# A chunkwise delta-rule recurrence on one core: the whole 64 x 64 inverse, four bursts of small products a chunk instead of five, and the last token tile of two heads transposed later

## The chip, the cores and the metric

One NeuronCore of one Trainium2 chip. The metric is the device time of one execution of the whole program in microseconds; the kernel before takes 772.99 us, the median of three runs (772.95 to 773.49). TensorE (PE in the rows; PEld is its weight load) does the products, VectorE (DVE) and ScalarE (ACT) the elementwise work and the reading of PSUM, SyncE (SP) and GpSimd (POOL) issue transfers. All arithmetic named here is float32; one float32 product shows as two instructions in the trace.

## The reference, cut to what matters

One layer of a decoder with two mixer branches (RWKV-7 and retention) and a hierarchical mixture of experts, for 528 prompt tokens (16 meta tokens and 512) and 8 sample tokens. The change touches the RWKV-7 recurrence over the prompt and the place of one small step of the retention branch:

```python
def rwkv_recurrence(r, w, k, v, kk, a, s0):
    def step(S, inp):
        r_t, w_t, k_t, v_t, kk_t, a_t = inp
        sa = jnp.einsum('bhvk,bhk->bhv', S, -kk_t)
        S = (S * w_t[:, :, None, :] + sa[..., None] * (kk_t * a_t)[:, :, None, :]
             + v_t[..., None] * k_t[:, :, None, :])
        y = jnp.einsum('bhvk,bhk->bhv', S, r_t)
        return S, y
...
scores = jnp.einsum('bihd,bjhd->bhij', q, k) * decay[None]
intra = jnp.einsum('bhij,bjhv->bihv', scores, v)
```

There are 8 RWKV heads of 64 channels and 4 retention heads of 128.

## The kernel before, in words

`order()` (from line 270) writes out one list of steps, `STEPS`, and each engine walks this list and does its own share of every step, in the list's order. So a step's place in the list is its place in the queue of every engine.

**The recurrence** works in chunks of 64 tokens (`CHUNKS`: eight full chunks and a last one of 16). Within a chunk the sequential rule becomes a triangular system: `sa` = (I - L)^-1 times a right side `rr`, with L strictly lower triangular, 64 x 64 for each head. The kernel inverts only the two 32 x 32 diagonal blocks (d = 0 and 1) of every head, by levels of doubling size: `wk_x` (line 1654) multiplies and `wk_t` (line 1667) updates, at levels 2, 4, 8 and 16, and after each of them DVE masks or adds the result from PSUM. The 8 heads x 2 blocks make 16 products of 32 x 32 for one `wk_x`. The block below the diagonal enters by substitution: `wk_sa` (1694) solves the upper half, `wk_y` (1704) multiplies it by the block below the diagonal (`below`), DVE adds that to `rr`, and `wk_sb` (1715) solves the lower half. `wk_r` (1681) makes the right side, `wk_s` (1723) the new state and the outputs, `wk_a` (1605) the chunk's score matrices, `wk_d` (1622) the raw diagonal blocks, `wk_k` (1638) the transposes. `wk_p` 0 to 5 (line 2393) are DVE's preparations of a chunk, `wk_e` three exponentials on ACT.

**Bursts and takes.** `bursts(c)` (line 360) groups the small products into five bursts for each chunk c, each with the work of c and of the one or two chunks ahead of it. Between two bursts stand `TAKES` = 3 pieces of large work ("takes"): halves of the gate and branch products at 128 x 128 x 260 (`j_f` at line 1438, `j_bb` at line 1415, in the first chunks `j_proj` at line 1402), some with DVE sums of weights (`fs`) ahead of them. `between` spreads the chunk's DVE and ACT steps over the takes. The loop starts at c = -2 with six takes ahead of it and two after each burst (`TAKES_AHEAD`), which is where the levels of chunks 0 and 1 are worked off, with the four sums `tg` of 128 x 1040 on DVE and eight small jobs `j_bon` of the bonus term.

**The retention heads** run earlier, behind the slots of a seven-product scheme (`j_w`, eight instructions at line 1457 for each slot, `seven(n, ...)`). Head h's steps stand at slots counted from `HEADS[h]` = 12, 22, 32, 42. `j_vt` and `j_kt` (1524) transpose the first four token tiles of v and k; `j_t4` (1518 to 1520) transposes the last, 24 rows with the last 16 prompt tokens and the 8 samples. `j_t4` waits for the rotated keys of its head (`rope`, on DVE, at the slots of `TURNS`: heads 0 to 3 at 7, 19, 31 and 39). It stands at slots 12, 22, 32 and 40. ACT reads its result, then POOL carries the sample rows out and back (`v_dram`, `v_all`) for `rs_v` on DVE at slots 18, 28, 38 and 46, and SP writes keys and values out (`kept`). These small jobs use PSUM banks 4 and 5 in turn: one may open when the last job but one has been read.

## Time and profile before

| | before |
|---|---|
| median of 3 runs | 772.99 us (772.95 to 773.49) |
| profiled execution | 773.59 us, span of its trace 771.9 us |
| PE busy | 740.1 us, 96% |
| DVE busy | 428.4 us, 56% |
| ACT busy | 229.5 us, 30% |
| retention heads and projections | about 26 to 254 us of the span |
| recurrence with the gate products between | about 257 to 503 us |
| branch and output products, routing | 503 to 619 us |
| experts, last rows | 619 to 772 us |

The page gives busy shares and the span in slices; the waits list who stood idle for whom; the timeline gives start and duration of merged instructions in order. A busy PE is not PE at its peak, since small products overlap and their latency counts as busy: so the cost of a group of small products is read from its start to the start of the next group.

### The profile page before, as it was taken

To read this page: it belongs to the slowest core of one execution; us is meant where nothing else is said; L and a number is where in the kernel's file an instruction comes from. 1 tells how busy PE (TensorE), PEld (TensorE's weight loads), DVE (VectorE), ACT (ScalarE), POOL (GpSimd) and SP (SyncE) were. 2 spreads that over 40 slices of the span, in tenths; PEclk is the share of its full clock that TensorE was granted. 3 is DMA by queue.
4 is the path that set the end of the run, shared out by engine and by line. 5 is a ranking of instruction groups with operands and counts; after the bars stand their busy time and mean duration, and the time that the engine had idled before them with its cause. 6 is when DMAs were issued, how large, how long until landed. Compare 5 with 4: busy or idle time off the path is not lost.

```text
span 771.9 us, 19753 instructions
## 1 busy us (share of the span) xinstructions
PE 740.1 (96%) x8328; PEld 527.0 (68%) x8328; DVE 428.4 (56%) x862; ACT 229.5 (30%) x543; POOL 45.3 (6%) x53
## 2 busy tenths in 40 slices
PE   7999999999999999999999999999999699999995
PEld 5887787787778777778878878778887533333331
DVE  5956667788787675756565564465223442212146
ACT  5122222254523333333323344310031501111145
POOL 0000000000000000010000000000000112221221
PEclk9999999999999999999999999999999689999998
DMA  9562432531221101121442102183934789999965
GB/s 324 205 207 85 155 126 72 209 114 56 73 91 56 56 30 58 58 59 44 148 119 59 57 30 84 44 332 122 409 125 167 250 349 397 392 402 390 377 211 220
DMA packets 38135, 130.43 MB, mean 169 GB/s; under 512 B 6267, under 2 KB 16763, under 8 KB 33184
## 3 DMA queue, kind: packets, MB, share of 16 engines
q1 hardware_dynamic: 32544, 115.07, 40.1%
q0 software_dynamic: 5504, 14.10, 6.2%
q8 instruction: 67, 1.10, 0.6%
q14 instruction: 20, 0.16, 0.1%
HBM read 111.13 MB, written 18.66 MB: 168 GB/s over the span
## 4 chain that ended last, share of the span: by engine, by line
PE 86%; DVE 5%; DMA 4%; issue 2%; ACT 1%; POOL 0%; SPq 0%; POOLq 0%; DVEq 0%; ACTq 0%
PE psum L1457 23%; PE psum L1812 11%; PE psum L1438 11%; PE psum L2784 9%; PE psum L2818 4%; PE psum L1415 4%; DVE arena L2184 3%; PE psum L1402 2%; PE psum L1390 2%; PE psum L1664 1%; PE psum L2764 1%; PE psum L1678 1%; PE psum L1580 1%; PE psum L1675 1%; DMA u_rows<-arena 1%
## 5 line engine op out<-in xcount | busy, mean ns | idle before, releaser
L2184 DVE TENSOR_TENSOR arena<-arena 128x268 f32<-128x268 f32 (+13 forms) x322 | 176.5, 548 | 47.6 <-ACT arena L1911 28.3
L1457 PE MATMUL psum<-arena 128*128 128x268 f32 x784 | 188.4, 392 | 0.0
L1457 PEld LDWEIGHTS psum<-arena 128*128 128x128 f32 x784 | 145.6, 190 | 33.0 <-issue 6.7
L1911 ACT ACTIVATE arena<-psum 128x268 f32<-128x268 f32 (+7 forms) x207 | 83.0, 410 | 258.9 <-PE psum L1457 138.6
L1911 ACT ACTIVATE arena<-arena 64x256 f32<-64x256 f32 (+11 forms) x173 | 69.0, 430 | 104.1 <-PE psum L1824 57.7
L1438 PE MATMUL psum<-arena 128*128 128x260 f32 x392 | 96.9, 392 | 0.8 <-DVE arena L2184 0.6
L2184 DVE TENSOR_TENSOR arena<-psum,arena 128x256 f32<-128x256 f32 (+7 forms) x151 | 60.4, 405 | 55.5 <-PE psum L1678 12.4
L1812 PE MATMUL psum<-arena 128*128 128x260 f32 x384 | 88.3, 385 | 1.5 <-DVE arena L2184 0.8
L2784 PE MATMUL psum<-arena 128*32 128x512 f32 (+1 forms) x640 | 86.7, 604 | 0.5 <-DVE arena L2949 0.3
L1438 PEld LDWEIGHTS psum<-arena 128*128 128x128 f32 x392 | 70.9, 189 | 17.3 <-issue 5.4
L1812 PEld LDWEIGHTS psum<-arena 128*128 128x128 f32 x384 | 71.3, 190 | 15.4 <-DVE arena L2187 2.1
L2949 DVE TENSOR_TENSOR arena<-psum,arena 128x256 f32<-128x256 f32 (+2 forms) x38 | 24.3, 663 | 102.1 <-ACT arena L2853 90.7
L2784 PEld LDWEIGHTS psum<-arena 128*32 128x32 f32 (+1 forms) x640 | 25.4, 117 | 58.2 <-issue 57.6
L2187 DVE SCALAR_TENSOR_TENSOR arena<-arena 128x536 f32<-128x536 f32 (+9 forms) x77 | 48.9, 635 | 7.7 <-ACT arena L1911 3.2
L2818 PE MATMUL psum<-arena 128*32 128x512 f32 (+1 forms) x288 | 40.2, 596 | 0.0
L2187 DVE SCALAR_TENSOR_TENSOR arena<-psum,arena 128x260 f32<-128x260 f32 (+2 forms) x23 | 10.2, 442 | 45.7 <-PE psum L1812 40.2
L1415 PE MATMUL psum<-arena 128*128 128x260 f32 x128 | 31.5, 390 | 0.0
L2184 DVE TENSOR_TENSOR arena<-arena,psum 128x260 f32<-128x260 f32 (+4 forms) x35 | 17.6, 514 | 20.5 <-PE psum L1438 16.8
L2853 ACT ACTIVATE arena<-psum 128x256 f32<-128x256 f32 x12 | 4.6, 384 | 78.8 <-PE psum L2784 78.8
L2187 DVE SCALAR_TENSOR_TENSOR arena<-arena,psum 128x260 f32<-128x260 f32 x32 | 13.7, 427 | 24.7 <-PE psum L1415 15.0
L1415 PEld LDWEIGHTS psum<-arena 128*128 128x128 f32 x128 | 23.2, 189 | 4.4 <-issue 0.4
L2818 PEld LDWEIGHTS psum<-arena 128*32 128x32 f32 (+1 forms) x288 | 10.8, 115 | 21.3 <-issue 21.3
(233 smaller groups left out, 669.0 us busy)
## 6 DMA issues: line engine op xcount, KB each, us to landing
arena<-in_w_gu SPq DMA_DIRECT2D x16, 2048.0 KB, 19.7
arena<-in_w_in SPq DMA_DIRECT2D x45, 512.0 KB, 4.2
arena<-in_w_dn SPq DMA_DIRECT2D x16, 1024.0 KB, 17.2
arena<-in_w_out SPq DMA_DIRECT2D x2, 2048.0 KB, 14.9
arena<-in_x SPq DMA_DIRECT2D x8, 268.0 KB, 6.0
arena<-arena SPq DMA_DIRECT2D x16, 134.0 KB, 4.4
arena<-in_x SPq DMA_DIRECT2D x1, 2144.0 KB, 14.5
arena<-arena SPq DMA_DIRECT2D x4, 520.0 KB, 6.5
```

The costliest lines, as they stand in the source:

```text
L1390: last = mm(ps, wt[:, i, k, :], xg[:, k, cols(hf)], start=(k == 0), stop=(k == KD - 1))
L1402: last = mm(ps, fill_in(0)[side][:, k // 2, k % 2, :], u[:, k, cols2(hf)], start=(k == 0), stop=(k == KD - 1))
L1415: last = mm(ps, bb_tile(m)[:, k, :], ret_o[:, k, cols2(hf)], start=(k == 0), stop=(k == NP - 1))
L1438: last = mm(ps, w[:, k // 2, k % 2, :], x[:, k, :], start=(k == 0 and i in (0, 1, 3)), stop=(k == KD // 2 - 1), skip_group_check=i not in ...
L1457: last = mm(ps, w[:, k, :], x[:, k, :], start=(k == 0 and i in (0, 1, 3)), stop=(k == KD // 2 - 1), skip_group_check=i not in (0, 1, 3))
L1812: last = mm(ps, w[:, k, :], x[:, k, cols2(hf)], start=(k == 0), stop=(k == nk - 1))
L1911: run(nc.scalar.activation(out, in_, fn, **kw), s)
L2184: run(v.tensor_tensor(out, a, b, op), s)
L2187: run(v.scalar_tensor_tensor(out, a, sc_, b, op0, op1), s)
L2784: last = mm(bank(2 + i % 2)[part], ue[:, i % 2, k, part], w_gu[x % NWE][:, k, :], start=(k == 0), stop=(k == KD - 1))
L2818: last = mm(bank(down_bank(e) + q)[part], hht(e)[:, f, part], w_dn[x % NWE][:, f, 512 * q:512 * q + 512], start=(f == 0), stop=(f == 1))
L2949: v.tensor_tensor(out, x, y, op).then_inc(s, 1)
```

## The change

In the recurrence the inverse becomes the whole 64 x 64 matrix. A fifth `wk_x` (level 32) multiplies the block below the diagonal by the upper inverse, a new step `wk_u` multiplies the lower inverse by that, and ACT assembles the pieces in `inv` (`wk_w` copies the two diagonal blocks in four instructions, `wk_u` the lower left one in two). `wk_sa` then solves a whole chunk with products of 64 x 64 x 64; `wk_y` and `wk_sb` and DVE's addition are gone. For full chunks `wk_t` at level 16 also keeps the other form of the upper block (eight more products). The bursts are regrouped into four for a chunk, with takes 4, 4, 3, 4 between them; the first levels of a chunk start one chunk earlier, the loop starts at c = -3 and `xl` and the PSUM places of `wk_x` and `wk_t` have two copies by the chunk's parity, so that PE no longer waits between two `wk_x` of one burst. DVE reads PSUM of `wk_x` or `wk_t` only after the last such product of the burst (and after `wk_d`, where it is in the burst). `wk_p` 0 to 4 of chunk c + 3 stand behind bursts 0 and 1 of chunk c, and `wk_d` of c + 3 in burst 2. In the heads, `j_t4` moves from slot 22 to 24 (head 1) and from 40 to 41 (head 3).

```diff
-TAKES = (3, 3, 3, 3, 3)
-TAKES_AHEAD, TAKES_LAST = 2, (3, 3, 2, 2, 2)
+TAKES = (4, 4, 3, 4)
+TAKES_FIRST, TAKES_AHEAD, TAKES_LAST = 4, 2, (3, 3, 2, 3)
...
-        then(b - 2 if h == RH - 1 else b, ("j_t4", h))
+        then((b, b + 2, b, b - 1)[h], ("j_t4", h))
...
-        return [of(c, ("wk_t", 16)) + of(c + 1, ("wk_x", 4)) + of(c, ("wk_r",)) + of(c + 1, ("wk_k",)),
-                of(c + 1, ("wk_t", 4)) + of(c, ("wk_sa",)),
-                of(c, ("wk_y",)) + of(c + 2, ("wk_d",)) + of(c + 1, ("wk_x", 8)),
-                of(c + 1, ("wk_t", 8)) + of(c + 2, ("wk_x", 2)) + of(c, ("wk_sb",)) + of(c + 1, ("wk_a",)),
-                of(c + 2, ("wk_t", 2)) + of(c + 1, ("wk_x", 16)) + of(c, ("wk_s",))]
+        return [of(c, ("wk_r",)) + of(c + 2, ("wk_x", 2)) + of(c + 1, ("wk_x", 8)) + of(c, ("wk_x", H)) + of(c + 1, ("wk_a",)),
+                of(c, ("wk_u",)) + of(c + 1, ("wk_t", 8)) + of(c + 2, ("wk_t", 2)),
+                of(c, ("wk_sa",)) + of(c + 1, ("wk_x", 16)) + of(c + 2, ("wk_x", 4)) + of(c + 3, ("wk_d",)),
+                of(c, ("wk_s",)) + of(c + 1, ("wk_t", 16)) + of(c + 2, ("wk_t", 4)) + of(c + 2, ("wk_k",))]
...
-    s += take(6)
-    for c in range(-2, len(CHUNKS) - 1):
+    s += take(TAKES_FIRST)
+    for c in range(-3, len(CHUNKS) - 1):
...
+        between = [of(c + 3, ("wk_e",)) + (prep(c + 2, ("wk_p", 5)) if c + 2 else []) + of(c + 1, ("wk_b",), ("wk_m",), ("wk_l",))
+                   + prep(c + 3, ("wk_p", 0)),
+                   prep(c + 3, ("wk_p", 1), ("wk_p", 2), ("wk_p", 3), ("wk_p", 4)),
+                   so[0:1], of(c + 1, ("wk_v",), ("wk_w",)) + so[1:3]]
+        for i, x in {-2: ((2, 0), (3, 1)), -1: ((1, 2), (2, 3))}.get(c, ()):
+            between[i].append(("tg", x))
...
                     for p, s, d, g, rd in tiles_of(c):
-                        last = mm(psum[g, 2304 + H * p:2304 + H * p + n], ad[c % 2][g, p, 0:n], tp[c % 3][g, 0, p, 0:n],
-                                  start=True, stop=True)
+                        if b == H:
+                            if d == 0:
+                                last = mm(psum[64 * s + H:64 * s + 64, 2560 + H * p:2560 + H * p + H], below[g, p, :],
+                                          tp[c % 3][g, 0, p, :], start=True, stop=True)
+                            continue
+                        o = 2304 + 128 * (c % 2) + H * p
+                        last = mm(psum[g, o:o + n], ad[c % 2][g, p, 0:n], tp[c % 3][g, 0, p, 0:n], start=True, stop=True)
...
+                elif kind == "wk_u":
+                    c = step[1]
+                    pe.wait_ge(s_xl, X_N[(c, H)])
+                    for p, s, d, g, rd in tiles_of(c):
+                        if d == 1:
+                            last = mm(psum[64 * s:64 * s + H, 3840 + H * p:3840 + H * p + H], tp[c % 3][g, 0, p, :],
+                                      tp[c % 3][g, 1, p, :], start=True, stop=True)
+                    last.then_inc(s_py, 1)
...
+                    if CHUNKS[c][1] == C:
+                        pe.wait_ge(s_y1, 6 * (c + 1))
+                        for p in range(NP):
+                            for s in range(2):
+                                _, _, full, _ = wk(c, s)
+                                last = mm(psum[full, 3328 + 64 * p:3328 + 64 * p + 64], inv[full, p, :], rr[full, p, :],
+                                          start=True, stop=True)
...
-                    dve.wait_ge(s_pt, X_N[(c, b)])
+                    dve.wait_ge(s_pt, X_RUN[(c, b)][1])
+                    for x in burst_of(step):
+                        if x[0] == "wk_d":
+                            dve.wait_ge(s_pab, PAB[x])
```

## Rows read from the trace of the kernel before

**Rows 1.** The page: busy time of PE and DVE, share of the span, instructions.
```profile
PE 740.1 (96%) x8328; PEld 527.0 (68%) x8328; DVE 428.4 (56%) x862; ACT 229.5 (30%) x543; POOL 45.3 (6%) x53
```
**Rows 2.** Windows: length, busy time by engine, granted clock, DMA share, GB/s.
```profile
306.00:503.00 197.00, 194.88 (x4270) 156.89 (x4264) 116.12 (x259) 70.47 (x183) 6.74 (x13) 1.00 0.23 70
619.00:738.00 119.00, 118.53 (x908) 42.09 (x908) 27.01 (x54) 15.89 (x27) 23.94 (x19) 0.98 0.97 376
```
**Rows 3.** Waits of PE: who waited for whom, us in total, times, longest.
```profile
PE psum L1520 <- issue: 3.0, 2, 1.5
PE psum L1678 <- DVE arena L2184: 1.1, 1, 1.1
```
**Rows 4.** Timeline of PE in chunks 4 and 5: start, duration, instructions, count.
```profile
388.35 0.68 PE L1742 MATMUL psum<-arena 64*64 64x64 f32 x16
388.96 2.90 PE L1415 MATMUL psum<-arena 128*128 128x260 f32 x12
391.79 0.45 PE L1678 MATMUL psum<-arena 32*32 32x32 f32 x32
392.07 0.48 PE L1664 MATMUL psum<-arena 32*32 32x32 f32 x32
...
397.32 0.64 PE L1701 MATMUL psum<-arena 32*32 32x64 f32 x16
397.90 2.90 PE L1438 MATMUL psum<-arena 128*128 128x260 f32 x12
400.73 0.64 PE L1712 MATMUL psum<-arena 32*32 32x64 f32 x16
401.29 0.45 PE L1631 MATMUL psum<-arena 64*32 64x32 f32 x32
```
**Rows 5.** The chain that ended last: a long run of large products without bursts.
```profile
254.92 4.38 PE psum L1402 x20
```
**Rows 6.** Timeline of chunk 5: DVE's work and the wait of PE behind it.
```profile
404.15 2.15 DVE L2184 TENSOR_TENSOR arena<-arena 128x512 f32<-128x512 f32 x3
404.99 1.12 PE L1438 MATMUL psum<-arena 128*128 128x260 f32 x4 [0.61 <-DVE arena L2184]
```
**Rows 7.** Timeline of the ahead stage: PE's waits, and the sums of 1040.
```profile
263.16 0.72 PE L1601 MATMUL psum<-arena 128*128 128x268 f32 x2 [0.26 <-DVE arena L2184]
276.46 1.23 DVE L2184 TENSOR_TENSOR arena<-arena 128x1040 f32<-128x1040 f32 x1
288.88 0.45 PE L1678 MATMUL psum<-arena 32*32 32x32 f32 x32 [1.10 <-DVE arena L2184]
```
**Rows 8.** Groups on DVE, 260 to 500 us: count, busy us, mean ns, idle before.
```profile
L2184 DVE TENSOR_TENSOR arena<-psum,arena 128x256 f32<-128x256 f32 x48 | 20.3, 426 | 27.9 <-PE psum L1678 10.5 <-PE psum L1742 8.5 <-PE psum L1664 4.4
L2184 DVE TENSOR_TENSOR arena<-psum,arena 128x128 f32<-128x128 f32 x45 | 13.2, 293 | 5.8 <-PE psum L1678 1.9 <-PE psum L1664 1.8 <-PE psum L1620 0.6
```
**Rows 9.** Timeline around `j_t4` of heads 2 and 3, with `rope` on DVE.
```profile
95.17 0.72 DVE L2184 TENSOR_TENSOR arena<-arena 128x536 f32<-128x536 f32 x1
95.99 0.60 PE L1520 MATMUL psum<-arena 128*24 128x128 f32 x4 [1.53 <-issue]
...
118.68 0.60 PE L1520 MATMUL psum<-arena 128*24 128x128 f32 x4 [1.43 <-issue]
122.28 0.55 POOL L1337 DMA_DIRECT2D arena<-v_smp  x1 [1.29 <-DMA v_smp<-arena]
...
134.31 1.22 DVE L2184 TENSOR_TENSOR arena<-arena 128x1024 f32<-128x1024 f32 x1
```
**Rows 10.** The page: a slot of the seven-product scheme is eight of these.
```profile
L1457 PE MATMUL psum<-arena 128*128 128x268 f32 x784 | 188.4, 392 | 0.0
```
**Rows 11.** Timeline around `j_t4` and `j_kt` of head 1.
```profile
68.01 0.62 PE L1520 MATMUL psum<-arena 128*24 128x128 f32 x4
...
73.23 0.60 PE L1524 MATMUL psum<-arena 128*128 128x128 f32 x4
73.49 1.07 DVE L2184 TENSOR_TENSOR arena<-psum,arena 128x256 f32<-128x256 f32 x2 [0.45 <-PE psum L1554]
```

More of the change, by code:

```diff
@@ L2064, in _ @@
                         act.wait_ge(s_act, own[0])
-                elif kind == "wk_b" and CHUNKS[step[1]][1] > H:
+                elif kind == "wk_b":
                     c = step[1]
@@ L2353, in _ @@
                 elif kind == "st0":
+                    for i in range(2):
+                        run(v.memset(inv[64 * i + H:64 * i + C, :, 0:H], 0.0))
                     job_done(dve, ("j_w", len(PAIRS) - 1, SEVEN - 1))
```

154 lines of the change are left out of this document (77 added, 77 removed).

## The prediction

> **What bounds the kernel now.** The first look is the page: PE is busy 96% of the span, DVE 56% [rows 1]. The second is the windows, because a share of the whole hides stages: in the recurrence, 306 to 503 us, PE is busy 194.9 of 197.0 us at a granted clock of 1.00 and DVE 116.1 [rows 2]. The third is the list of waits of PE. Before 600 us it holds few entries, and two bear on this change: 3.0 us in two waits at line 1520, which is `j_t4`, and 1.1 us at line 1678, `wk_t`, behind DVE [rows 3]; single waits of 0.61 and 0.26 us behind DVE stand in the timeline [rows 6, 7]. So the recurrence is bound by what PE has to push through, not by the chain of dependences: the five bursts and fifteen takes of a chunk follow each other nearly without a gap. A change there is worth what it takes off PE's queue, less the waits that it makes. A step counts from its start to the next start, since the durations of small products overlap: 32 instructions of 32 x 32 last 0.45 us by the record, but the next group starts 0.28 us later [rows 4].
>
> **The change part by part.** The time is summed against the profiled span of 771.9 us; that execution took 773.59 us, 0.6 above the median of 772.99, to which the difference is applied.
>
> (1) Products removed, for each of the eight full chunks. `wk_sa` on the upper half is 16 instructions of 32 x 32 x 64, from 397.32 to 397.90, 0.58 us. `wk_y` has the same shape, 400.73 to 401.29, 0.56 us. `wk_sb` has it too, and I take it at the same 0.56 [rows 4]. Together 1.70 us.
>
> (2) Products added, for each of the same chunks. The new `wk_sa` has 16 instructions of 64 x 64 x 64, the shape of line 1742: 388.35 to 388.96, 0.61 us [rows 4]. Level 32, `wk_u` and the extra half of `wk_t` at level 16 are 16 instructions of 32 x 32 x 32 each, on two of the four row groups. No row shows such a half group. From below: half the instructions of a full group, half of its 0.28 us, 0.14. From above: each row group works off its own eight instructions one after the other, as in the full group, so the half group takes as long, 0.28. The row that it is nearest to is line 1701, also 16 instructions on two row groups, with twice the columns: half of its 0.58 is 0.29 [rows 4]. I take 0.28, so three cost 0.84 (0.42 from below). Added: 0.61 + 0.84 = 1.45 us.
>
> At this place the Trainium skill speaks against the change. In "TensorEngine Tiling (Array Packing)", section Restrictions and Gotchas, it says that different row tiles cannot access the same PSUM bank simultaneously; all products of one of these groups write one bank. By that the sixteen would run one by one. The row stands against it: 32 products' instructions on four row groups go to one bank in 0.28 us, 9 ns each, where one large instruction of 260 columns takes 219 ns, so that 32 columns in their share of it would alone be 27 ns; four together are needed to come to 9 [rows 4, 5]. By the rule the three half groups would cost 3 x 16 x 27 ns = 1.30 us instead of 0.84 and the sum would be 3.7 us smaller; the measurement decides, and I leave it out.
>
> (3) One burst fewer. Twelve large instructions without a burst take 12 x 4.38 / 20 = 2.63 us [rows 5]. Between two bursts they take 391.79 - 388.96 = 2.83 and 400.73 - 397.90 = 2.83 [rows 4]. So each change from small products to large and back costs 0.20 us; the number of large instructions is the same (15 takes a chunk before and after). Minus 0.20 us a chunk. Changes of shape inside the bursts are about as many as before and are left at nothing, with 0.1 a chunk to either side in the range.
>
> (1) to (3): -1.70 + 1.45 - 0.20 = -0.45 us a chunk, eight times: -3.6 us. With half groups at 0.14 it is -0.87 a chunk, -7.0 us.
>
> (4) DVE and ACT in the recurrence. DVE loses one addition of 128 x 256 (426 ns) a chunk and gains a copy of 128 x 128 (293 ns), and the level-16 update is 256 instead of 128 wide (+133 ns) [rows 8]: no change. ACT loses two reads and gains four short copies and two more, hidden, since it is busy 70.5 of 197 us [rows 2] and they stand a burst ahead of who needs them: `wk_w` is queued on ACT behind the last take of burst 3, ahead of the read of `wk_r`, which PE needs only in burst 2. That cover would have to shrink from about 10 us to under 2 to cost anything. The distances between the links of the chain (`wk_r`, `wk_sa`, `wk_s`, back to `wk_r`) grow from three takes to eight, three and four. What gets closer is `wk_d` of chunk c + 3: it waits for `wk_p` 4 of that chunk, which DVE meets only behind the last take of burst 1. Ahead of `wk_d` PE has in burst 2 `wk_sa`, `wk_x` 16 and `wk_x` 4, 0.61 + 0.28 + 0.28 = 1.17 us; DVE has in that time the subtraction or product of the take and `wk_p` 4, two operations of 0.43 with a gap, about 1.0 us. It is covered, by little. Then DVE waits in burst 2 for `wk_d` before it reads `wk_x` 16, and behind it queue `wk_x` 4, the three operations of `wk_d` and the next sums `fs`. A wait of PE for such sums exists already, 0.61 us behind three operations of 128 x 512 [rows 6]. Such waits I take as many as before; bounds -0.8 (the 0.61 goes and none comes) and +3 us (one of 0.4 us in each of seven chunks).
>
> (5) The ahead stage. It has eight bursts with two takes each where it had nine, -0.2 us; the number of takes ahead of the first `wk_r` is 4 + 2 + 8 + 8 = 22, as before (6 + 6 + 10). DVE is closer to full here: behind burst 1 of c = -1 stand four `wk_p` (4 x 0.43), a `tg` of 1.23 us and two `wk_t` (2 x 0.43), 3.8 us with the gaps near 4.2, in a stretch of PE of about 1.2 us of burst and 2 to 2.6 us of takes. So `wk_d` of chunk 2 is late by some 0.5 us, and at c = -2 `wk_d` of chunk 1 and a `j_bon` behind it by some 1.1 us together. Against that goes the wait of 1.10 us at line 1678 in the old order, and the 0.26 stays [rows 7]. Net +0.5 us; bounds -1.1 and +2.
>
> (6) `j_t4`. PE waits at it for heads 2 and 3, 1.53 and 1.43 us, and for head 1 not at all [rows 9, 11]. At head 2 the rotation of the keys ends on DVE at 95.89 and PE starts at 95.99. The diff leaves head 2 where it is. Head 3 moves one slot of eight large products back, 8 x 188.4 / 784 = 1.92 us [rows 10], more than the 1.43; the rotation then is done, and PE's bank has been read. Gain 1.43 us; bounds 0 (the wait goes to the next small job) and -1.5. It is past no queue that has no room: POOL sent the samples' rows out at 122.28 and the product that needs them runs on DVE at 134.31, 12 us later, of which two go [rows 9]. SP's `kept`, its two writes, comes later by the same and ahead of loads that are asked for two pairs early. Head 1 moves from slot 22, where it cost no wait, to 24, between a score and `j_kt`. With the bank order then `j_kt` opens on the score's bank. DVE starts to read that score at 73.49, ends at about 73.92, and `j_kt` could start at about 73.75 [rows 11]: +0.2 us; bounds 0 and +0.5.
>
> **Sum:** -3.6 + 0 - 0.2 + 0.5 - 1.43 + 0.2 = -4.5 us. I take -4.2, since in (4) a little more can come than go: 773.0 - 4.2 = 768.8 us. What follows, to the end of the routing, is bound by PE as well or starts from PE's steps. The experts' stage has DMA at 0.97 with PE busy 118.5 of 119.0 us [rows 2]: its loads start when PE frees their buffers, so they move with PE, and the gain is kept.
>
> **The rivals.** A, the half groups are cheap: 0.14 us each, -0.87 a chunk; -7.0 - 0.2 + 0.5 - 1.4 + 0.2 + 0.3 gives 765.4 us. For it speaks that 32 instructions need no longer than 0.28 us; against it line 1701.
>
> B, the gain is eaten by new waits behind DVE in bursts 0 to 2 and in the ahead stage, at their upper bounds in part: +3 us against -4.2 gives 771.8 us, no difference that a measurement of this kernel tells from none (0.2%, 1.5 us). For it speaks that DVE is busy 59% of the stage and that its reads now wait for the last product of a burst; against it, that its longest lag in the steady chunks shows once.
>
> C, slower: `wk_d` waits for `wk_p` 4 in every chunk. The place is burst 2. If DVE reaches `wk_p` 4 one operation of 128 x 512 (0.7 us) later than I have it, and the operations behind it (`wk_x` 16, three of `wk_d`, `fs`) push the wait on to a take, PE loses 0.7 us at `wk_d` and about 0.3 behind it, nine times: +9 us against -4.2 gives 777.8. It decides from 0.6 us a chunk on: there nine waits are worth 5.7 us, the 4.2 and the 1.5 of the bound. Against it: DVE's total is not raised.
>
> D, the change doesn't do what it says at the heads: the wait of head 3 goes elsewhere, to the score or `j_ros` behind it, and head 1 costs 0.5: +1.7, 770.5 us. It lies in the forecast's range.
>
> **How the numbers follow.** The forecast with D in it has 0.57, A 0.15, B 0.17, C 0.11. Faster by over 0.2% (under 771.4 us) are the forecast and A: 0.72, less 0.01 for the forecast's edge; within 0.2%: B and the edge, 0.17; slower 0.12. The range: A at 765.4 reaches to about 764.8 with a tenth beyond; on the other side B is inside and most of C outside, 773.5.
>
> **What would show it.** The timeline of a steady chunk: `wk_sa` of 64 x 64 from start to next start 0.6 us; `wk_u` 0.28 (A: 0.14); twelve or sixteen large instructions 0.2 us above 0.219 each; the period of a chunk 0.45 us shorter. In PE's waits: line 1520 with one wait of 1.5 instead of two; line 1524 new with 0.2; waits at line 1631's successor (`wk_d`) behind DVE under 0.3 us in sum in the steady chunks (C: 0.7 each). The prediction is wrong if PE's waits behind DVE or ACT between 254 and 503 us come to over 5 us, or if a new step waits for instructions rather than for data.

## The result: 23 us slower, and the profile after

The changed kernel takes 795.93 us (median of four runs, 791.96 to 798.99) beside 772.97 us for the kernel before on the same chip (four runs, 772.35 to 773.49): 1.0293 times the time, 95% interval 1.0261 to 1.0324. The prediction was 768.8 us in a range of 764.8 to 773.5. Its profiled execution is its longest run, 798.99 us, with a span of 797.3 us; before it was 771.9 us. The 25.4 us between the two spans are what the traces have to account for. Three single executions that took 1.6 times as long or more (one of the run with a take inside the burst, two of the kernel before) are left out of all medians and ratios below.

The page of the changed kernel, the rows for PE and DVE and the two that carry instructions (queue, kind, packets, MB, share):

```profile
PE 748.4 (94%) x8456; PEld 532.6 (67%) x8456; DVE 429.0 (54%) x864; ACT 237.0 (30%) x575; POOL 44.9 (6%) x53
...
q8 instruction: 68, 1.11, 0.6%
q14 instruction: 20, 0.16, 0.1%
```

DVE works as long as before [rows 1]; PE is busy for a smaller share of a longer span. The windows (length, PE busy, granted clock, DMA share, GB/s) of the stage ahead and of the recurrence:

```profile
254.00:306.00 52.00, 47.10 (x1153) 1.00 0.13 39
306.00:503.00 197.00, 181.77 (x4099) 0.97 0.23 68
```

In the recurrence PE stands idle for 15.2 of 197 us where it was 2.1 [rows 2], and the clock is 0.97 where it was 1.00. For whom it waits there, 254 to 530 us, in total, times, longest (the largest entries):

```profile
PE psum L1635 <- issue: 5.4, 4, 1.6
PE psum L1665 <- issue: 3.0, 2, 2.6
PE psum L1698 <- issue: 2.7, 1, 2.7
PE psum L1432 <- ACT arena L1926: 2.0, 1, 2.0
PE psum L1646 <- DVE arena L2215: 2.0, 2, 1.7
PE psum L1455 <- DVE arena L2212: 0.9, 1, 0.9
PE psum L1683 <- DVE arena L2458: 0.9, 1, 0.9
PE psum L1455 <- issue: 0.8, 1, 0.8
```

Most of it is "issue", 12.6 of 20.5 us: no semaphore ended it. Line 1635 is `wk_a`, 1662 and 1665 are `wk_k`, 1694 and 1698 `wk_t`, 1646 and 1650 `wk_d`, 1679 and 1683 `wk_x`, 1432 and 1455 are takes. The timeline shows what is odd about these stalls (start, duration, line, operation, shape, count, idle before):

```profile
404.23 0.63 PE L1662 MATMUL psum<-arena 128*64 128x128 f32 x4
404.69 0.49 PE L1665 MATMUL psum<-arena 128*128 128x128 f32 x3
407.80 0.33 PE L1665 MATMUL psum<-arena 128*128 128x128 f32 x1 [2.62 <-issue]
407.97 3.70 PE L1432 MATMUL psum<-arena 128*128 128x260 f32 x16
411.60 0.69 PE L1719 MATMUL psum<-arena 128*64 128x64 f32 x16
412.21 0.75 PE L1683 MATMUL psum<-arena 32*32 32x32 f32 x64
412.82 0.44 PE L1679 MATMUL psum<-arena 32*32 32x32 f32 x16
413.19 0.94 PE L1635 MATMUL psum<-arena 64*128 64x128 f32 x12
415.29 0.49 PE L1635 MATMUL psum<-arena 64*128 64x128 f32 x4 [1.16 <-issue]
```

They fall inside a step: between the third and fourth instruction of `wk_k`'s second half, behind the twelfth of sixteen of `wk_a`. In the code no wait stands inside these loops, so no data is awaited there.

A count over the trace says where they fall. All records of PE's stream are numbered from 0, in order of time: matmuls, weight loads and the 535 waits and other instructions of its sequencer. Each product in this kernel's code is four (two loads, two matmuls), a transpose two. By these numbers the stalls of over 0.3 us that the list calls "issue" end, from 254 to 530 us, at 193 or 194 above a multiple of 256. Instructions come in packets of 16384 bytes (1.11 MB in 68 packets on queue 8, above). The stream has 17,447 records; 68 packets of 256 instructions would be 17,408, at 64 bytes each, so queue 8 is read here as PE's. The packets' times beside the times at which PE passes these places ("borders"), taken from the records of the trace. These are nine of the borders; where there is a stall, the time is its end:

```
passed at us   line   us since the last fetch began   us until the next began   stall there
 364.13        1694   4.23                            1.82                      -
 369.41        1683   3.46                            1.16                      -
 374.42        1757   3.85                            0.23                      -
 377.17        1665   2.53                            5.60                      0.35
 385.14        1635   2.37                            1.24                      1.56
 402.62        1757   2.43                            2.57                      -
 407.80        1665   2.61                            4.85                      2.62
 415.29        1635   2.64                            1.75                      1.16
 435.52        1455   2.46                            4.66                      0.84
```

Over all twenty traces of this case there are 111 such stalls between 254 and 530 us, of 0.3 to 4.2 us. All end at 193 to 195 above a multiple of 256, though the kernels' streams differ, and each ends 2.2 to 3.2 us behind the beginning of a fetch. The two waits at `j_t4` that the list also calls "issue" end at other numbers (126 and 99 in the kernel before). So PE stands still for its own instructions. It does so at one border in eight: PE passes some 890 in these stretches, and in the changed kernel nine of 44 have a stall. In a burst of small products PE goes from border to border in some 2 to 3 us (402.62 to the stall behind 404.69 above), a fetch needs 2.2 to 3.2 us to be of use, and the next one begins behind a border, 0.2 to 2.8 us in most cases; right behind a burst's end, with takes following, it began 4.7 to 5.6 us later. In the kernel before the same list had two entries of the kind, which I had read past:

```profile
PE psum L1652 <- issue: 1.1, 1, 1.1
...
PE psum L1675 <- issue: 0.5, 1, 0.5
```

The Trainium skill, "Runtime: NRT & Kernel Launch", section Instruction fetch mechanics, says that instructions are refilled in blocks of 256 and that the sequencer fetches the next page while it executes the current one. The packets agree. It also says that crossing such a boundary is mostly hidden. By count that is so here (35 of the 44 borders), but the nine others cost 0.3 to 2.7 us each, 12.6 us together.

The second part of the loss is the clock. Around the stall at 304.8 to 307.6 us, and behind it:

```profile
306.00:308.00 2.00, 0.44 (x22) 0.75 0.86 281
308.00:313.00 5.00, 5.00 (x17) 0.50 0.13 37
```

PE was idle for 2.72 us, and the granted clock goes to 0.50, that is 1.2 instead of 2.4 GHz; the takes in it run at half speed. The same stands behind the stall at 443.10:

```profile
443.10 0.49 PE L1635 MATMUL psum<-arena 64*128 64x128 f32 x3 [1.34 <-issue]
443.51 4.58 PE L1432 MATMUL psum<-arena 128*128 128x260 f32 x12
```

Twelve large instructions take 4.58 us where they took 2.90 [rows 4]. The kernel before has no such stretch in the recurrence. The changed kernel has three there, 13.7 us together, and one of 3.4 us at 98.80 us, in the heads' stage, behind the wait of 1.5 us at head 2's `j_t4` that the kernel before has too [rows 9].

**The sum**, from the records of both traces. Idle time is that between PE's first and last instruction. "At borders": idle stretches of PE of over 0.25 us at the places above, 254 to 530 us. "Half speed": half of the time at 0.50, which is what it costs if PE has work all the while. "Rest": span less this idle time less half speed, that is PE's work at the full clock and some 14 us ahead of PE's first instruction and behind its last. The differences are of the unrounded values.

| us | before | after | difference |
|---|---|---|---|
| idle at borders, 254 to 530 us | 1.5 | 12.6 | +11.1 |
| other idle time, 254 to 530 us | 4.6 | 7.8 | +3.3 |
| idle elsewhere | 11.4 | 14.3 | +2.8 |
| half speed | 12.4 | 20.8 | +8.5 |
| rest | 742.0 | 741.7 | -0.3 |
| span | 771.9 | 797.3 | +25.4 |

Of the half-speed term 6.8 us belong to the recurrence and 1.7 to the stretch at 98.80 us. The idle time elsewhere grew behind 530 us, in the routing and at the experts' first products; why is open.

### The profile page after: what moved, and what is told of

It is laid out like the page before. It is cut to its first block, busy times and chain, and to the rows that moved or that the text cites. A ratio compares the mean times of both kernels' runs of the same rounds, so it can differ in the third digit from the quotient of the medians.

```text
span 797.3 us, 20050 instructions
## 1 busy us (share of the span) xinstructions
PE 748.4 (94%) x8456; PEld 532.6 (67%) x8456; DVE 429.0 (54%) x864; ACT 237.0 (30%) x575; POOL 44.9 (6%) x53
## 3 DMA queue, kind: packets, MB, share of 16 engines
q8 instruction: 68, 1.11, 0.6%
## 4 chain that ended last, share of the span: by engine, by line
PE 81%; DVE 6%; DMA 5%; issue 4%; ACT 3%; SPq 0%; POOL 0%; POOLq 0%; DVEq 0%; ACTq 0%
PE psum L1474 20%; PE psum L1455 11%; PE psum L1827 11%; PE psum L2817 9%; DVE arena L2212 4%; PE psum L1432 4%; PE psum L2851 3%; DMA arena<-u_rows,ids 2%; PE psum L1407 2%; PE psum L1698 1%; PE psum L1683 1%; ACT arena L1926 1%; PE psum L1635 1%; PE psum L2797 1%; PE psum L1694 1%
## 5 line engine op out<-in xcount | busy, mean ns | idle before, releaser
L2212 DVE TENSOR_TENSOR arena<-arena 128x268 f32<-128x268 f32 (+12 forms) x322 | 176.5, 548 | 48.3 <-ACT arena L1926 28.5
L1474 PEld LDWEIGHTS psum<-arena 128*128 128x128 f32 x784 | 146.6, 191 | 33.9 <-issue 7.0
L1926 ACT ACTIVATE arena<-psum 128x268 f32<-128x268 f32 (+7 forms) x223 | 87.5, 400 | 267.0 <-PE psum L1474 140.4
L1926 ACT ACTIVATE arena<-arena 32x128 f32<-32x128 f32 (+9 forms) x205 | 78.2, 410 | 119.4 <-PE psum L1839 57.7
L1455 PE MATMUL psum<-arena 128*128 128x260 f32 x392 | 99.9, 403 | 1.8 <-DVE arena L2212 0.9
L2212 DVE TENSOR_TENSOR arena<-psum,arena 128x128 f32<-128x128 f32 (+6 forms) x143 | 58.3, 411 | 70.4 <-PE psum L1698 14.2
L1827 PE MATMUL psum<-arena 128*128 128x260 f32 x384 | 88.3, 385 | 1.5 <-DVE arena L2212 0.8
L1455 PEld LDWEIGHTS psum<-arena 128*128 128x128 f32 x392 | 74.0, 196 | 17.8 <-issue 5.7
L1827 PEld LDWEIGHTS psum<-arena 128*128 128x128 f32 x384 | 71.2, 189 | 15.5 <-DVE arena L2215 2.1
L1432 PE MATMUL psum<-arena 128*128 128x260 f32 x128 | 32.9, 405 | 2.0 <-ACT arena L1926 2.0
L1432 PEld LDWEIGHTS psum<-arena 128*128 128x128 f32 x128 | 24.5, 199 | 7.1 <-ACT arena L1926 2.4
L2215 DVE SCALAR_TENSOR_TENSOR arena<-arena,psum 128x260 f32<-128x260 f32 x32 | 13.7, 427 | 26.8 <-PE psum L1432 17.1
## 6 DMA issues: line engine op xcount, KB each, us to landing
arena<-in_w_out SPq DMA_DIRECT2D x2, 2048.0 KB, 15.2
arena<-in_x SPq DMA_DIRECT2D x1, 2144.0 KB, 15.6
```

The source lines that it names most:

```text
L1432: last = mm(ps, bb_tile(m)[:, k, :], ret_o[:, k, cols2(hf)], start=(k == 0), stop=(k == NP - 1))
L1455: last = mm(ps, w[:, k // 2, k % 2, :], x[:, k, :], start=(k == 0 and i in (0, 1, 3)), stop=(k == KD // 2 - 1), skip_group_check=i not in ...
L1474: last = mm(ps, w[:, k, :], x[:, k, :], start=(k == 0 and i in (0, 1, 3)), stop=(k == KD // 2 - 1), skip_group_check=i not in (0, 1, 3))
L1827: last = mm(ps, w[:, k, :], x[:, k, cols2(hf)], start=(k == 0), stop=(k == nk - 1))
L1926: run(nc.scalar.activation(out, in_, fn, **kw), s)
L2212: run(v.tensor_tensor(out, a, b, op), s)
```

## The experiments

Theory F: PE starves for instructions at the borders, and the clock falls behind some of the stalls. Rival D: the stalls belong to the new steps themselves (banks, row tiles, a wait that the trace misattributes). Later the question was how much is the longer bursts (B) and how much the place where the borders fall (P); L says that the kernel before had a lucky place.

### The instruction stream moved: empty instructions

```diff
+            for _ in range(64):          # 128, 192 in the others
+                pe.nop(nofuse=True)
             pe.wait_ge(s_set, 1)
```

> The changed kernel with 64 empty instructions at the head of TensorE's program, where it waits for the first loads anyway; nothing else differs. Theory (blocks): TensorE's instructions come in blocks of 256 (queue 8 moved 68 packets and 1.11 MB, 16 KB each), all long waits marked issue end at the same place modulo 256, and a block that is used up in the time of a dense burst, under about 3.5 us, is followed by a wait for the next. A chunk of the changed kernel has 5 blocks of instructions almost exactly, so the two bad borders (in wk_k and in wk_a) come back in every chunk. Shifted by 64 only one border a chunk should be bad: 783 to 790 us, waits in wk_a at lines 1635 to 1637 gone. Rival (dependences: semaphores, a busy VectorE): nothing moves, 792 to 799 us.

> As the one before with 128 empty instructions. Theory (blocks): the waits move to other lines, about two borders a chunk are bad again (inside burst 2 and in the first half of burst 3): 790 to 800 us, but none of the waits in wk_a. Rival (dependences): the same waits at the same lines, 792 to 799 us.

> As the one before with 192 empty instructions. Theory (blocks): waits move again, to burst 1 and burst 2, 786 to 800 us. Rival (dependences): no change, 792 to 799 us. If the three shifts and the changed kernel lie within 2 us of each other, the theory of blocks is wrong.

Measured: 795.55, 792.91 and 795.12 us; 1.0305 (1.027 to 1.034), 1.0295 (1.024 to 1.035), 1.0301 (1.026 to 1.034). The empty instructions appear nowhere in the traces, and every stall ends at the number it had. So nothing was shifted, and these runs say nothing on the theories, though their numbers fit the rivals. They are of use as repeats of the changed kernel. The third of them and the changed kernel (span and granted clock):

```profile
core 0: 788.0 us, clock 0.988
```
```profile
core 0: 797.3 us, clock 0.975
```

The order of instructions is the same, PE's idle time too (35.0 and 34.7 us in all), but the first spent 20.6 us at half speed and the second 41.6. Half of the 21.0 is 10.5 us, and the spans differ by 9.3. So the spread of the changed kernel's runs is mostly the clock, and not each stall brings a half-speed stretch: this run has none in the recurrence, with nearly the same stalls (11.3 us at borders beside 12.6).

### One half alone: the two heads

The kernel before with only the places of `j_t4` changed.

```diff
-        then(b - 2 if h == RH - 1 else b, ("j_t4", h))
+        then((b, b + 2, b, b - 1)[h], ("j_t4", h))
```

> The kernel before with only the new places of j_t4 (heads 1 and 3). The prediction's step: minus 1.4 us for head 3, plus 0.2 for head 1, 771.8 us. Rival: the wait of head 3 goes to another job, 772.5 to 773.2. The theory of blocks: no instruction is added, two waits may be, so the phase of the recurrence stays and nothing of the 23 us shows here.

Measured: 773.66 us, 1.0004 (0.9989 to 1.0020). Its waits of PE from 60 to 254 us:

```profile
PE psum L1520 <- issue: 1.5, 1, 1.5
PE psum L1524 <- DVE arena L2184: 0.5, 1, 0.5
PE psum L1573 <- DVE arena L2184: 0.4, 1, 0.4
```

Head 3's 1.43 us at line 1520 are gone [rows 3, 9], and `j_kt` of head 1 (1524) waits 0.5 us for DVE. That leaves 0.9 us, less than this comparison can tell from none.

### The stream moved in truth: additional small products

Each product is four instructions in PE's stream, so n additional ones ahead of the first step move all that follows by 4n places.

```diff
                         pe.wait_ge(s_sq, KD * hf + k + 1)
+                        for _ in range(32 if (hf, k) == (0, 0) else 0):     # 64 in the other
+                            mm(ps[0:H, 0:1], ones[:, 0:H], squares[:, 0, 0:1], start=True, stop=True)
                         for i in range(4):
```

The expectations count two instructions for each product; the shifts were 128 and 256 places, as the numbers of the stalls show, not 64 and 128 as written in them.

> The changed kernel with 32 additional one-column matmuls (64 instructions, about 0.6 us) ahead of the first matmul of the norm's first step, so that every later instruction of TensorE stands 64 places further in its stream. The empty instructions of the runs before did not appear in the stream, so this is the first real shift. Theory F (TensorE starves for instructions: all unexplained stalls end at the same place of a block of 256 instructions, behind a late instruction fetch): the borders of the blocks now fall 64 instructions earlier in each chunk, in the middle of the t4 step with another border 256 dense instructions ahead of it, and at the end of the group of x steps. One bad border a chunk is left where there were two: the stalls move to other steps (the end of t4 instead of k and wk_a), their sum in 290 to 475 us falls from about 15 us to 6 to 10, and the time is 784 to 791 us. Rival D (the stalls belong to the steps: shared PSUM banks, row tiles of the half groups, or a wait for data that the trace misattributes): same steps, same lengths, 793 to 799 us.

Measured: 796.34 us, 1.0294 (1.0265 to 1.0323). PE's waits, and one of them in the timeline:

```profile
PE psum L1652 <- issue: 10.6, 5, 2.6
```
```profile
398.18 0.39 PE L1652 MATMUL psum<-arena 64*32 64x32 f32 x21
401.16 0.31 PE L1652 MATMUL psum<-arena 64*32 64x32 f32 x11 [2.59 <-issue]
401.40 4.58 PE L1432 MATMUL psum<-arena 128*128 128x260 f32 x12
```

(Line 1652 here is line 1650 of the changed kernel, `wk_d`.) The stalls left `wk_k` and `wk_a` and went to `wk_d`, which had none in the steady chunks, in five chunks; a sixth stands in `wk_t`. Their numbers in the stream are 5570, 6850, 8130, 9410, 10689 and 10946: still 193 or 194 above a multiple of 256.

> The changed kernel with 64 additional one-column matmuls at the same place (128 instructions, about 1.2 us): all later instructions stand 128 places further. Theory F: no burst now holds two borders, and no border stands right ahead of the takes; the unexplained stalls in 290 to 475 us fall from about 15 us to 2 to 6, none of them in wk_a or k, and the clock has no stretch at half speed in the recurrence; 778 to 787 us. Rival D: same steps and lengths as in the changed kernel, 794 to 800 us.

Measured: 797.65 us, 1.0312 (1.0273 to 1.0352):

```profile
PE psum L1637 <- issue: 4.9, 4, 1.6
PE psum L1667 <- issue: 2.6, 1, 2.6
PE psum L1700 <- issue: 2.2, 1, 2.2
```

Moved by one whole block the stalls are back in the steps and at nearly the sizes of the changed kernel (lines 1635, 1665, 1698 there), 10.0 us together. That is what F says of 256 places, and D cannot say why 128 should empty these steps and 256 fill them. D is out. F's forecasts of time missed all the same: 784 to 791 and 778 to 787 us were expected. That of fewer stalls, made for a shift of 128, is answered by the run before, where the sum at the borders stayed 11.9 us; a shift of 64 in truth comes below.

### Five bursts instead of four

```diff
-TAKES = (4, 4, 3, 4)
+TAKES = (3, 3, 3, 3, 3)
...
-                of(c, ("wk_s",)) + of(c + 1, ("wk_t", 16)) + of(c + 2, ("wk_t", 4)) + of(c + 2, ("wk_k",))]
+                of(c, ("wk_s",)) + of(c + 2, ("wk_k",)), of(c + 1, ("wk_t", 16)) + of(c + 2, ("wk_t", 4))]
```

(from chunk 0 on; `TAKES_LAST` is (3, 2, 2, 2, 2))

> The changed kernel, all its steps and sums as they are, but its last burst (s, t16, t4, k: about 336 instructions of TensorE) split in two: s and k, then three takes, then t16 and t4, with three takes behind each of the five bursts instead of 4, 4, 3, 4. Theory F: the longest run of dense instructions falls from 336 to about 290; two fetches in a burst disappear; stalls without a releaser in 290 to 475 us fall from about 15 us to 2 to 7, and the time is 775 to 785 us (the additional burst costs 0.2 us in each of 8 chunks). Rival D: the same sum of stalls, 794 to 800 us. Rival W (the waits for VectorE and ScalarE are the loss): these were 5 us in the changed kernel; fewer takes between dependent steps raise them, over 800 us.

Measured: 787.37 us, 1.0179 (1.0145 to 1.0214); borders 3.6 us. The stalls are within F's 2 to 7 us, the time is 2.4 us above its range. Rival W (over 800 us) is out. The rest looked like F's case, until the same kernel was moved by 128 places with the additional products:

> The kernel with five bursts, and 32 one-column matmuls (128 instructions, 0.6 us) ahead of the norm's first, so that the borders of the blocks of 256 instructions lie half a block away from where they lay. It has no burst over 290 instructions. Theory F: the 2.2 us stall in the stage ahead (t at 306.8 us, right behind a late fetch) and the 0.5 to 0.9 us ones at wk_a and t leave those places; others of 0.5 to 2.5 us may come where a border now falls behind a late fetch; their sum in 290 to 475 us stays at 2 to 7 us, far under the 15 us of four bursts: 781 to 790 us. If the phase were what made five bursts cheap (rival P), the stalls would come back to 10 us or more: over 792 us.

Measured: 794.16 us, 1.0272 (1.025 to 1.0294); borders 9.7 us, where F had 2 to 7. The rival P had set 792 as its mark: the place of the borders, not the five bursts, had made most of the gain.

### The recurrence alone

The changed kernel with the old places of `j_t4`.

> The changed kernel with the last token tile of heads 1 and 3 transposed at its old place: the inverse and the bursts alone. The heads alone made 1.0004 of the time of before, so by every theory this is the changed kernel's time within 0.4%: 792 to 799 us; that the two parts work on each other (the head's steps move where the blocks of instructions end) would show as a difference over 3 us.

Measured: 795.09 us, 1.0289 (1.0256 to 1.0322). The whole loss is the recurrence's.

### The same mechanism in the kernel before

The kernel before with 32 additional products of one column in each chunk: all ahead of x16 in the longest burst, or 16 ahead of x4 and 16 ahead of x8.

```diff
                     n = min(CHUNKS[c][1], H)
+                    for p, s, d, g, rd in tiles_of(c)[0:4] * (8 if b == 16 else 0):     # (4 if b in (4, 8) else 0)
+                        mm(psum[g, 2304:2305], ad[c % 2][g, 0, 0:n], tp[c % 3][g, 0, 0, 0:1], start=True, stop=True)
                     for p, s, d, g, rd in tiles_of(c):
```

> The kernel before, with 32 additional one-column products of 32 x 32 tiles (128 instructions of TensorE; their results are overwritten by the step's own) ahead of the x16 step of each chunk, in its longest burst (t2, x16, s: about 291 instructions, then about 419). None of the change is in it. The work added is 8 chunks x 32 products x about 20 ns = 5 us. Theory F (TensorE's instruction fetch: a burst in which a whole block of 256 instructions is used up faster than the next is fetched starves): of 8 bursts of 419 instructions about five hold two borders of blocks, each with a stall of 1 to 2.7 us that no releaser ends, inside s or x16; 773 + 5 + 5 to 13 = 783 to 791 us. Rival D (stalls belong to the new kernel's steps or banks): 5 us of work and no stall, 777 to 779 us.

> The control of the run before: the same 32 products in each chunk, 16 ahead of x4 in the first burst (181 to 245 instructions) and 16 ahead of x8 in the third (227 to 291), so that no burst is longer than the kernel before has one already. The same work, 5 us. Theory F: stalls as few as in the kernel before (1.6 us in two), or up to 3 us: 777 to 781 us, and at least 5 us under the dense one. Rival D: equal to the dense one within 1 us.

Measured: dense 803.0 us, 1.0395 (1.037 to 1.042); spread 790.91 us, 1.0224 (1.020 to 1.0248). The waits of the dense one:

```profile
PE psum L1744 <- issue: 6.7, 2, 4.2
PE psum L1733 <- issue: 3.2, 1, 3.2
PE psum L1739 <- issue: 2.5, 1, 2.5
PE psum L1666 <- issue: 1.3, 1, 1.3
```

Lines 1733 to 1744 are `wk_s`, a step that the change does not touch, behind x16 in the lengthened burst. So the kernel before, without anything of the change, falls into the same stalls (14.3 us at borders) once work is added to its burst, and the same work put elsewhere costs 12 us less. The 12 us are not the price of the longer burst alone: each run shows one place of the borders, and the place by itself is worth more than that in other kernels (below). Both took more than F's figure (783 to 791, and 777 to 781). In the spread one the borders cost 7.7 us (up to 3 us were expected), the half-speed term 13.9, and the rest is 748.9, that is 6.9 us above before for the added work where I had 5. No burst was over 291 instructions there, as in the kernel before: that length alone is no limit under which nothing happens.

### A take inside the longest burst

```diff
-            s += now_
+            inside = int(i == 3 and 0 <= c < len(CHUNKS) - 2 and c != 5)
+            s += now_[:1] + take(1) + now_[1:] if inside else now_
```

(and one take fewer behind that burst)

> The changed kernel with one of the four takes behind its last burst of chunks 0 to 4 and 6 moved into that burst, behind s: no additional work, the same order of all else, the same place in the instruction stream from the burst's end on. Theory F: the stalls inside that burst (k 2.6, 0.7 and 0.4 us, t16's 2.7 us is of the stage ahead and stays) go, as a take of 0.9 us lies between its two borders; those of wk_a in the next burst (1.2 to 1.6 us, four times) have their border where they had it, three takes behind k's end instead of four, and stay or grow: stalls without a releaser in 315 to 475 us fall from about 10 to 4 to 8 us, 789 to 794 us. Rival P (phase alone decides, not the dense run): k's stalls stay, 793 to 799 us.

Measured: 794.84 us (median of three), 1.0279 (1.025 to 1.0308); the borders cost 9.4 us instead of 12.6:

```profile
PE psum L1636 <- issue: 4.8, 4, 1.9
PE psum L1699 <- issue: 2.7, 1, 2.7
PE psum L1663 <- issue: 1.9, 1, 1.9
```

`wk_k`'s stall did not go, as F had it, but stands at 1.9 us, and `wk_a`'s stayed. The stalls of 315 to 475 us sum to 6.7 us, inside F's 4 to 8, and the time is within P's 793 to 799. But the kernels with the same recurrence and nothing moved scatter as much: 6.4 to 9.5 us in that window, with `wk_k`'s largest stall at 1.2 to 2.4 (the empty instructions, the recurrence alone). So this run decides nothing. One take of 0.9 us inside is less than the fetch's delay.

### How much is the place of the borders

From one `wk_s` to the next PE's stream has 1276 or 1277 records in the changed kernel, nearly five blocks (1280), so a border stands in the same step of one chunk after the other: the stalls in `wk_a` are at 7362, 8641, 9922 and 11202. In the kernel before it is 1243 to 1245, and the borders drift by some 36 a chunk. These runs move both kernels by 64, 128 or 192 places with the additional products (16, 32 or 48 of them).

> The kernel before with 16 one-column matmuls (64 instructions, 0.3 us) ahead of the norm's first: nothing else is changed. Its chunk has about 1250 instructions, so the borders of the blocks of 256 drift by some 30 from chunk to chunk and meet each place of a burst at most once or twice. Theory F: its two small stalls (1.1 and 0.5 us) go or move, others of that size may come: 772 to 777 us. If the kernel before merely had a lucky phase (rival L), it loses 5 us or more: over 778 us.

> The same with 32 one-column matmuls (128 instructions, 0.6 us). Theory F: 772 to 778 us; rival L: over 778 us.

> The changed kernel with 16 one-column matmuls at the same place (64 instructions): the borders lie in its last burst twice a chunk, about 20 instructions behind its beginning and 256 later, in t4's second half. Its chunk is 5 x 256 instructions, so that is so in each chunk. Theory F: stalls of 2 to 2.7 us without a releaser at the end of t4 or at k in four or five chunks, none in wk_a; 10 to 14 us between 290 and 475 us, 792 to 798 us. If this were the lucky phase (rival L), less than 5 us of stalls and under 786 us.

> The changed kernel with 48 one-column matmuls (192 instructions): the borders lie twice in its second burst (u, t8, t2: 290 instructions), at its beginning and near its end. Theory F: stalls of 2 to 2.5 us in t2's second half in four or five chunks, none in k or wk_a; 8 to 14 us between 290 and 475 us, 789 to 797 us. Rival L: under 786 us.

> The kernel with five bursts, moved by 64 instructions. With shifts of 0 and 128 it took 787.4 and 794.2 us, the changed kernel with its four bursts 796 and 796, and 785.9 and 808.4 with shifts of 64 and 192. If the four longer bursts cost time of themselves (B), five bursts are below four in the mean over the four phases, by 5 us or more: 780 to 788 us here. If only the phase counts (P), the mean of both is alike, 795 to 797: as 787 and 794 lie below it, then 797 to 808 us here or with the shift of 192.

> The kernel with five bursts, moved by 192 instructions; its longest burst (u, t8, t2: 290 instructions) is the one that held two borders in the changed kernel at this shift (808.4 us). B: the last two bursts are short, but this one is as before: 788 to 798 us. P: 798 to 808 us.

Measured, medians in us, with the idle time at borders (254 to 530 us) of the profiled run in brackets:

| moved by | before | four bursts (the change) | five bursts |
|---|---|---|---|
| 0 | 773.0 (1.5) | 795.9 (12.6) | 787.4 (3.6) |
| 64 | 778.2 (3.6) | 785.9 (4.5) | 786.6 (6.4) |
| 128 | 779.4 (1.8) | 796.3 (11.9) | 794.2 (9.7) |
| 192 | not run | 808.4 (15.6) | 806.6 (13.5) |
| mean | 776.9 | 796.6 | 793.7 |

The ratios to before: 1.0067 (1.0044 to 1.009) and 1.0079 (1.0053 to 1.0106) for before moved by 64 and 128; 1.0188 (1.0135 to 1.0242) and 1.0459 (1.042 to 1.0498) for four bursts at 64 and 192; 1.0163 (1.0117 to 1.021) and 1.0426 (1.0375 to 1.0478) for five. The waits of the changed kernel moved by 64, and then by 192:

```profile
PE psum L1700 <- issue: 4.0, 2, 2.7
```
```profile
PE psum L1700 <- issue: 8.0, 4, 2.1
PE psum L1648 <- issue: 5.7, 2, 3.6
```
```profile
391.75 0.38 PE L1700 MATMUL psum<-arena 32*32 32x32 f32 x22
394.26 0.33 PE L1700 MATMUL psum<-arena 32*32 32x32 f32 x9 [2.13 <-issue]
394.52 6.72 PE L1432 MATMUL psum<-arena 128*128 128x260 f32 x16
```

The places came as forecast: t4's second half at 64, the end of t2 at 192 (the timeline). The sizes did not: 64 has two large stalls and not four or five, and meets L's mark of a lucky place instead (under 5 us of stalls, under 786 us); 192 has more than forecast, and 16 large instructions behind one of them take 6.72 us, partly at half speed, where 3.70 is usual. Where the borders fall is worth 22 us in the changed kernel and 20 in the one with five bursts; the three places of before lie within 6.4 us. The kernel before was at its best of the three: it passes L's mark of 778, by 0.2 and 1.4 us. But its stalls explain little of the 5 and 6 us: at borders it has 2.0 us more when moved by 64, and 0.2 more when moved by 128, where the spans of the profiled runs are 3.1 and 4.9 us longer. In the first half speed costs 2.7 us less, in the second the idle time elsewhere is 2.2 us longer, and PE's work is 3.2 and 2.0 us longer, more than the 0.3 and 0.6 expected for the added products; what makes that is open. Four bursts against five is 2.9 us in the mean, with 786 against 787 at the best place, so the number of bursts as such is the smaller part; B's 5 us were not met, and P's 797 to 808 came at 192.

The changed kernel moved by 64 shows one thing more. It has only 3.0 us more at borders than the kernel before and its span is still 12.1 us longer: 4.0 are other idle time between 254 and 530 us, 3.4 half speed, 1.8 idle time elsewhere, and PE's work is the same within 0.2. So even where the borders do little harm, the forecast's gain is not there.

No version beat the kernel before. Why the changed kernel has more stalls than the kernel before in the mean over the places is not isolated.

## Why the prediction was wrong, point by point

**What bounds the kernel.** "The recurrence is bound by what PE has to push through" was read rightly from [rows 2, 4]; the step from there to "a change there is worth what it takes off PE's queue, less the waits that it makes" failed, because the waits that I went through were those behind DVE and ACT. The supply of PE's own instructions is none of them: it was put at nothing, and it measured 11.1 us more at borders and, with the granted clock that fell behind some of the stalls, 6.8 us of half speed in the recurrence. The two small "issue" waits at 1652 and 1675 were in the list that I read, and `j_t4`'s "issue" at 1520 had another cause (DVE's rotation [rows 9]), which made it easy to take the word for a semaphore in general.

**(1) Products removed, 1.70 us a chunk.** Start to start over 254 to 530 us, less idle time, `wk_sa`, `wk_y` and `wk_sb` of the eight full chunks together were 13.16 us, 1.64 for each. Right.

**(2) Products added, 1.45.** The new `wk_sa` is

```profile
424.65 0.68 PE L1730 MATMUL psum<-arena 64*64 64x64 f32 x16
425.26 0.75 PE L1683 MATMUL psum<-arena 32*32 32x32 f32 x64
```

0.61 us, as forecast, and 0.61 in the mean of the eight. The half groups overlap with their neighbours, so they are read as what `wk_x` and `wk_t` cost more over the stage: level 32 0.23, the extra half at level 16 0.45; `wk_u` costs 0.20. That is 0.88 together where 0.84 was taken. So the half groups are not cheap (rival A, 0.14 each). The rule of the Trainium skill on row tiles and one PSUM bank ("TensorEngine Tiling (Array Packing)", Restrictions and Gotchas), by which the prediction had each at 0.43, fits one of the three at most. Added in all 1.49 a chunk.

**(3) One burst fewer, -0.20.** Sixteen large instructions take 3.70 us, 0.20 above 16 x 0.219 [rows 5]. Right. So (1) to (3) by these measurements are -0.35 a chunk, -2.8 us. But `wk_a` costs 1.5 us more over the stage and `wk_k` 0.5 (less idle time), which I had at nothing. In the changed kernel moved by 64 and by 128, where no stall stands in `wk_a`, `wk_a` costs 9.1 us as in the kernel before, so its 1.5 us come with the stalls. The work term of -3.6 us is -0.3 in the table of sums. The same term scatters by some 3 us among the kernels with the same work (741.5 to 745.5), so I can say that it is small, not that it is zero.

**(4) Waits behind DVE and ACT in the recurrence, 0, bounds -0.8 and +3.** A wait of 2.0 us at 475.28, behind ACT, was new:

```profile
475.28 1.15 PE L1432 MATMUL psum<-arena 128*128 128x260 f32 x4 [2.03 <-ACT arena L1926]
```

It stands in every run with four bursts and in none of the other runs; those with five have one of 1.5 us behind ACT at 512 to 530 us. Of (4) and (5) together the idle time away from the borders grew by 3.3 us; mine was +0.5, within bounds of -1.9 and +5. Rival C (`wk_d` late for `wk_p` 4 in every chunk) did not come: the long waits of `wk_d` with a releaser are in the stage ahead.

**(5) The stage ahead, +0.5, bounds -1.1 and +2.** A `wk_d` waits 1.71 us for DVE at 290.19, another 0.26, a `wk_x` 0.92 and a `j_bon` product 0.68, against the 1.10 and 0.26 of before [rows 7]: +2.2 us. The mechanism was named, the size was just over the upper bound.

**(6) The heads, -1.2.** Head 3's wait went, as forecast. Head 1 costs 0.5 instead of 0.2. Alone it is 1.0004 of the time.

**The rivals and the range.** C ended slower, by 5 us, for a reason that did not occur (its nine waits of 0.6 us are 5.4 us, not the 5.7 that it names; nothing hangs on it). None of the cases had PE short of instructions or at half speed, so the range was too narrow at the upper end by 22 us. Both signs that I had named for a wrong prediction came: the waits behind DVE and ACT between 254 and 503 us pass 5 us (5.8 in the rows shown above, and two smaller entries of 0.7 and 0.6; about half of it ahead of 306 us), and steps wait for instructions.

**What stays open.** What delays the beginning of a fetch is not settled: 0.2 to 2.8 us behind a border in most cases, near 5 where takes follow at once. Other transfers are not the cause in at least one case: a fetch began at 440.18, 4.7 us behind its border, the stall at 443.10 followed, and in between

```profile
435.50:440.10 4.60, 4.58 (x74) 1.00 0.00 0
```

no data moved (share 0.00). Around the stall at 304.8 us the DMA share was 0.86 (window 306 to 308 us, above), and whether that lengthened it is open. Nor is it settled why the same stalls bring half-speed stretches in one run and none in another. That a chunk of nearly 1280 instructions is a trap by itself is argued from the table, not shown: no run changed the chunk's length alone.

## What to carry to other kernels

Count PE's instructions and not only its time: bursts of small fp32 products use up a block of 256 instructions in 2 to 3 us, about what its fetch takes, so what a regrouping costs depends on where the borders fall, and can be more than the products that it saves. A loop whose body is nearly a whole number of blocks can be expected to meet a bad place each time or never (argued, not shown). Before a change of 1 or 2% is judged, move the stream by 64, 128 and 192 instructions with a few tiny products and look at all four times. In the list of waits, an "issue" inside a step without a semaphore can be this stall: look at its number in the stream.

## What the runs showed of the hardware

- A stall for instructions ends 2.2 to 3.2 us behind the beginning of a fetch (median 2.5, 111 stalls in 20 traces); single ones cost 0.3 to 4.2 us. With no other change than 16 to 48 tiny products ahead of the first step, the kernel took 785.9 to 808.4 us.
- Behind an idle time of PE of over 1 us in the midst of dense work the granted clock can go to 0.50 (1.2 GHz). In the 20 traces it did so 39 times between 254 and 530 us, 34 times behind a stall for instructions (of 78 over 1 us) and five times behind a wait of 1.5 to 2.0 us for DVE or ACT; the stretches in the recurrence lasted 3.4 or 6.8 us: 12 large instructions then take 4.58 us instead of 2.90. Two profiled runs of the same order of instructions spent 20.6 and 41.6 us at half speed, with spans of 788.0 and 797.3 us.
- Empty instructions put into PE's program left no trace in its stream and moved nothing; products of one column do, four instructions each.
- Sixteen instructions of 32 x 32 x 32 on two row groups cost 0.20, 0.23 and 0.45 us (the last two as differences of whole steps), where 32 on four take 0.28.
